# Hybrid decoder layer with routed experts: the end as products for gathered rows and last experts, smaller tiles, quarter refills, and unread products on TensorE while routing is worked out

## The chip, the cores and the metric

One core of a Trainium2 chip runs the whole program. The metric is the device time of one execution in microseconds; of several runs the median is given. Beside it one execution was profiled, and all rows below are from that one.

## The reference

One layer of a decoder on 512 tokens of width 1024 in float32: a mixer with four head groups, then a mixture of experts, then a last norm. The change touches only the mixture and what follows it:

```
lg = t @ w_rg + b_rg                       # 4 groups, the best one is taken
le = (t @ w_re + b_re) inside that group   # 4 experts, the best two are taken
w1, w2 = softmax weights of the two, times that of the group
y = sum over the two of  w * ((silu(t @ w_gate[e]) * (t @ w_up[e])) @ w_down[e])
x = x + g2 * y
out = rms_norm(x, final_norm)
```

Here `t` is the normed and modulated `x` (512 x 1024), `w_gate[e]` and `w_up[e]` are 1024 x 512 and `w_down[e]` is 512 x 1024. There are 16 experts, so each token's two rows make 1024 rows in all, spread unevenly over the experts.

## The kernel before

Each engine has its own instruction stream, written out by hand, with semaphores between them. The mixture begins in `pe_moe`, `act_moe`, `dve_moe`, `pool_moe` and `sync_moe`, with one function for each step of an expert. In what follows P = 128, ST = 4 (token tiles), KT = 8, E = 16.

**Routing.** For each of the four token tiles TensorE makes the output projection, transposes `x2` (L1196) and multiplies with the routing weights (L1203). Then VectorE picks group and experts (L1342 to L1381) and signals `before_tile`; TensorE counts how many rows of each expert stand before each token (L1208, L1209: the rank products); VectorE turns this into places (L1388 to L1447). The rows of the first expert are taken by products with 0/1 matrices (L1215), since they are on the chip; VectorE and ScalarE modulate them (`dve_rows`, `act_rows`, L1110 and L1078), and the first expert's products begin. For the other experts POOL gathers rows from DRAM by a list (L1540).

**Ranks and tiles.** The experts 0, 1 and 2 are pinned to the ranks 0 to 2 so that their weights can be loaded before routing is known. The others are ranked by their count of rows. A rank has a fixed number of rows, `SIZES`: 128 for ranks 0 to 7, 64 for 8 to 11, 32 for 12 to 15. What doesn't fit goes to up to 12 extra tiles of 128 rows behind the experts, each run only if it is needed (`extras`). `ORDER` is the order in which ranks are computed: 0, 1, 2, 14, 3, 13, 4, 12, 5, 11, 6, 10, 7, 9, 8, 15. "n" below is the place in that order.

**One expert.** `pe_gate_up` (L1031, small tiles L1025) makes gate and up, ScalarE the silu, VectorE the product, `pe_hidden` (L1041) transposes, `pe_down` (L1064, small tiles L1059) multiplies with the down weights, `dve_output` (L1131, L1135) multiplies with the gate `g2` into `yo`, and `act_output` (L1100) stores `yo` in DRAM. In TensorE's order the gate and up products of n come before the down products of n - 1, except for the last n.

**Weights.** SP loads them into three buffers. Gate and up of n wait for the gate and up products of n - 3, the down weights for the down products of n - 3. Only for n = 3 are gate and up loaded in quarters, each when a quarter of the first expert's products is done (L962); for all others L898. All weight loads are in one queue and are served in its order.

**The end.** When all stores but the last are through, POOL gathers each token's first row from DRAM (`y1`, four gathers, L1552), and after the last store its second (`y2`). VectorE adds `w1 * y1` (L1515) and `w2 * y2` (L1521), ScalarE makes the sum of squares (L1312) and the root (L1314), VectorE the mean (L1525), the reciprocal and the last product (L1528), and SP sends the tile out (L986). `fnb` (L974) is the last norm's weight.

## Time and profile before

| | us |
|---|---|
| median of 3 runs | 781.9 (779.35 to 783.69) |
| the profiled execution: time | 781.9 |
| the profiled execution: span | 780.0 |
| TensorE busy | 686.8 (88%) |
| VectorE busy | 318.2 (41%) |
| ScalarE busy | 180.0 (23%) |
| GpSimd busy | 116.7 (15%) |
| mean granted TensorE clock | 0.946 |
| first expert's products begin | 489.56 |
| last expert's products end | 747.95 |

The span is the time from the first to the last instruction; the time of an execution is 1.9 us longer. Engines: PE is TensorE (PEld its weight loads), DVE VectorE, ACT ScalarE, POOL GpSimd, SP the engine that only issues transfers; a name with q (SPq, ACTq) is that engine's sequencer. Busy shares are averages over stages with different limits, so one stage is read at a time. A float32 product shows as two records. A granted clock of 1.00 is 2.4 GHz, 0.50 is 1.2 GHz. DMA is the mean busy share of the 16 DMA engines; it can show a little over 1.

### The profile page before, as it was taken

How to read it: one execution, taken by the hardware profiler on the slowest of the kernel's cores; microseconds unless marked ns; L12 is line 12 of the kernel's file. 1: busy time of each engine (PE TensorE's matmuls, PEld its weight loads, DVE VectorE, ACT ScalarE, POOL GpSimd, SP SyncE). 2: the span in 40 equal slices, each digit the busy share in tenths (PEclk: the TensorE clock that was granted, in tenths of full speed). 3: DMA queues.
4: the chain of work that ended last, by engine and by line, in shares of the span. 5: the costliest groups of instructions: out<-in, count | busy, mean ns of one | idle time of the engine just before them, and what ended most of it. 6: DMA issues, size and time to landing. Idle time of an engine off the chain costs nothing.

```text
span 780.0 us, 9903 instructions
## 1 busy us (share of the span) xinstructions
PE 686.8 (88%) x3851; PEld 401.5 (51%) x3851; DVE 318.2 (41%) x752; ACT 180.0 (23%) x434; POOL 116.7 (15%) x164
## 2 busy tenths in 40 slices
PE   1799899999999999879999985899999999999830
PEld 1674446667666697545654455444444544443210
DVE  3203657856466533786612228350211211202126
ACT  3204215122121121456711141020111211201103
POOL 8700122313032155000000000010000000000030
PEclk9989999999999999899999986999999999999975
DMA  9999003793330300750085047638999999999965
GB/s 332 375 264 364 3 1 108 245 294 109 108 108 1 52 5 7 266 216 2 1 324 108 28 179 280 195 110 349 375 423 413 405 413 409 390 404 410 421 208 201
DMA packets 75475, 173.62 MB, mean 223 GB/s; under 512 B 21954, under 2 KB 38940, under 8 KB 71836
## 3 DMA queue, kind: packets, MB, share of 16 engines
q1 hardware_dynamic: 69520, 157.59, 56.0%
q0 software_dynamic: 2672, 9.44, 3.5%
q10 hardware_dynamic: 3228, 5.84, 2.0%
q8 instruction: 37, 0.61, 0.3%
q14 instruction: 18, 0.15, 0.1%
HBM read 156.59 MB, written 16.26 MB: 222 GB/s over the span
## 4 chain that ended last, share of the span: by engine, by line
PE 76%; DVE 9%; POOL 4%; issue 4%; ACT 3%; DMA 3%; POOLq 0%; ACTq 0%; DVEq 0%
PE ps L1031 14%; PE ps L1153 7%; PE ps L1064 7%; PE ps L2300 7%; PE ps L2267 5%; PE ps L1025 4%; PE ps L1059 2%; PE ps L2378 2%; PE ps L2264 2%; PE ps L2384 2%; DMA expert_rows<-yo 2%; PE ps L2291 2%; POOL lev L1648 2%; PE ps L653 2%; PE ps L2388 2%
## 5 line engine op out<-in xcount | busy, mean ns | idle before, releaser
L1031 PE MATMUL ps<-gu,xgT 128*128 128x512 f32 x256 | 113.0, 600 | 3.6 <-DVE xgT L1110 2.5
L1031 PEld LDWEIGHTS ps<-gu,xgT 128*128 128x128 f32 x256 | 48.6, 192 | 63.2 <-issue 63.2
L2300 PE MATMUL ps<-hT,winr 128*128 128x512 f32 x144 | 72.6, 612 | 0.0
L1540 POOL DMA_INDIRECT xg<-xn_rows,list x15 | 13.9, 928 | 384.7 <-DVE list L1447 185.9
L1153 PE MATMUL ps<-wout,yT 128*128 128x512 f32 x128 | 57.6, 610 | 0.0
L1064 PE MATMUL ps<-dn,hidT 128*128 128x512 f32 x128 | 56.5, 594 | 0.0
L1753 POOL TENSOR_TENSOR cc<-low,lev 128x512 f32<-128x512 f32 x20 | 30.2, 1518 | 129.5 <-DVE low L2087 104.0
L1891 DVE SCALAR_TENSOR_TENSOR acc<-ada,st,acc 128x512 f32<-128x512 f32 x56 | 48.5, 866 | 1.3
L2267 PE MATMUL ps<-hT,wind 128*128 128x512 f32 x96 | 43.4, 605 | 0.0
L1025 PE MATMUL ps<-gu,xgT 128*32 128x256 f32 (+1 forms) x384 | 43.0, 452 | 0.0
L1153 PEld LDWEIGHTS ps<-wout,yT 128*128 128x128 f32 x128 | 24.6, 195 | 30.0 <-issue 30.0
L1120 DVE TENSOR_TENSOR hidm<-sg,ps 128x512 f32<-128x512 f32 x8 | 5.5, 687 | 84.3 <-ACT sg L1085 84.3
L1085 ACT ACTIVATE sg<-ps 128x512 f32<-128x512 f32 (+2 forms) x16 | 7.4, 464 | 135.3 <-PE ps L1031 102.9
L1064 PEld LDWEIGHTS ps<-dn,hidT 128*128 128x128 f32 x128 | 23.7, 190 | 26.9 <-issue 26.8
L2300 PEld LDWEIGHTS ps<-hT,winr 128*128 128x128 f32 x144 | 24.0, 192 | 14.3 <-issue 12.3
L2267 PEld LDWEIGHTS ps<-hT,wind 128*128 128x128 f32 x96 | 18.4, 196 | 20.8 <-issue 20.7
L1135 DVE TENSOR_TENSOR yo<-ps,g2m 128x512 f32<-128x512 f32 x16 | 10.3, 687 | 45.3 <-PE ps L1064 27.8
L1025 PEld LDWEIGHTS ps<-gu,xgT 128*32 128x32 f32 (+1 forms) x384 | 16.7, 119 | 22.8 <-issue 18.0
L727 DVE TENSOR_REDUCE st<-ps 128x1 f32<-128x256 f32 (+3 forms) x48 | 20.3, 451 | 18.4 <-PE ps L660 18.3
L2101 DVE TENSOR_TENSOR uu<-uu,ps 128x512 f32<-128x512 f32 x20 | 13.7, 686 | 32.9 <-PE ps L2384 32.8
L1059 PE MATMUL ps<-dn,hidT 128*32 128x256 f32 (+1 forms) x192 | 24.0, 474 | 3.4 <-ACT hidT L1090 3.4
L780 ACT ACTIVATE pr<-ps,st 128x256 f32<-128x256 f32 (+3 forms) x48 | 23.5, 492 | 14.1 <-DVE st L727 14.1
(433 smaller groups left out, 1046.6 us busy)
## 6 DMA issues: line engine op xcount, KB each, us to landing
dn<-in_w_down SPq DMA_DIRECT2D x16, 2048.0 KB, 23.3
gu<-in_w_gate SPq DMA_DIRECT2D x15, 2048.0 KB, 21.5
gu<-in_w_up SPq DMA_DIRECT2D x15, 2048.0 KB, 26.0
ada<-in_w_ada SPq DMA_DIRECT2D x12, 2048.0 KB, 11.6
expert_rows<-zero SPq DMA_DIRECT2D x12, 512.0 KB, 6.7
expert_rows<-yo ACTq DMA_DIRECT2D x8, 512.0 KB
wout<-in_w_out SPq DMA_DIRECT2D x1, 3072.0 KB, 10.6
x<-in_x SPq DMA_DIRECT2D x2, 1024.0 KB, 6.2
```

Of the source, the lines that this page charges most:

```text
L653: t.matmul(PS[n][:, 0:nk], q[pb, pr, i * P:(i + 1) * P], keys[pb, 0, j0 * P:j0 * P + nk], start=True, stop=False)
L727: ins = v.tensor_reduce(m, PS[n][:, 0:nk], AX.X, ALU.max, negate=True)
L780: a.activation(T["pr"][:, u % PRS, 0:nk], PS[n][:, 0:nk], ACT.Exp, bias=m, accum_out=den[:, c:c + 1]).then_inc(sem("exp"), 1)
L1025: ins = nc.tensor.matmul(PS[2 * b][m * s:m * s + m, 0:2 * f].rearrange("p (w f) -> p w f", w=2), T["xgT"][:, k, 0:m], w_in[:, :, k, s * f: ...
L1031: ins = nc.tensor.matmul(PS[2 * b + w][:, :], T["xgT"][:, k, :], w_in[:, w, k, :], start=(k == 0), stop=(k == KT - 1))
L1059: ins = nc.tensor.matmul(PS[4][m * w:m * w + m, 0:d], T["hidT"][:, c, m * s:m * s + m], w_in[:, f, w * d:(w + 1) * d], start=(f == 0), sto ...
L1064: ins = nc.tensor.matmul(PS[4 + w][:, :], T["hidT"][:, f, :], w_in[:, f, w * 512:(w + 1) * 512], start=(f == 0), stop=(f == FT - 1))
L1153: ins = nc.tensor.matmul(PS[2 * (i % 2) + n][:, :], T["yT"][:, k, i * P:(i + 1) * P], T["wout"][:, k, n * 512:(n + 1) * 512], start=(k == ...
L1753: g.tensor_tensor(CC[lv % 2][:], T["low"][:], T["lev"][:, lv].unsqueeze(1).broadcast_to([P, H, P]), ALU.mult).then_inc(sem("cc"), 1)
L1891: ins = v.scalar_tensor_tensor(o, piece[:, k, :], csil[:, k:k + 1], o, ALU.mult, ALU.add)
L2267: ins = t.matmul(bank[:, :], w(k), T["hT"][:, k, :], start=(k == 0), stop=(k == KT - 1))
L2300: ins = t.matmul(bank[:, :], w(k), T["hT"][:, k, :], start=(k == 0), stop=(k == KT - 1))
```

## The change

- **Tile sizes.** `SIZES` is 128 for ranks 0 to 6, 64 for 7 to 11, 32 for 12 to 15. The last three in the order are the ranks 13, 14 and 15: the order is 0, 1, 2, 12, 3, 11, 4, 10, 5, 9, 6, 8, 7, 13, 14, 15. Up to 13 extra tiles.
- **Last three experts on chip** (`on_chip`). Their outputs go into the tile `yc` (96 rows) and are neither stored nor gathered.
- **The end as products** (`pe_back`). For each token tile TensorE adds up, in two PSUM banks, diag(w1) times `y1`, diag(w2) times `y2`, and a 0/1 matrix with weights (`back`) times `yc`: six products of 128 x 512. VectorE adds the result to `x2`. `back` is made by VectorE (`in_row`), transposed by TensorE (`pe_onehot`) and copied by ScalarE during the expert loop.
- **Gathers.** `y1` is gathered once the stores up to n = 11 are through and the gate and up products of n = 13 are done, `y2` after the store of n = 12.
- **Quarter refills** for n = 3, 4 and 5.
- **Unread products** (`keep_busy`): 11 products of 128 x 512 ahead of the rank products, 3 ahead of the first expert's row products, 3 ahead of its gate and up products. Nothing reads what they give.
- **Small steps.** The mean and epsilon of the norms move from VectorE into ScalarE's root; the root's table is loaded ahead of the last norm; the extra tiles' branches stand inside one outer branch; one more tile of zeros and a 64-row one are written to DRAM early.

```diff
-SIZES = [128] * 8 + [64] * 4 + [32] * 4
+SIZES = [128] * 7 + [64] * 5 + [32] * 4
+CHIP = 3
+_big, _less = list(range(NBUF, BIG)), list(range(E - CHIP - 1, BIG - 1, -1))
+while _big:
+    ORDER += [_less.pop(0), _big.pop(0)]
+ORDER += _less + list(range(E - CHIP, E))
+ONEHOT_AT = 3
...
-                if n == NBUF:
+                if n < 2 * NBUF:
+                    b = n - NBUF
                     for part in range(4):
                         if part < 3:
-                            sp.wait_ge(sem("first_gu_mm"), part + 1)
+                            sp.wait_ge(sem("first_gu_mm"), 3 * b + part + 1)
                         else:
-                            sp.wait_ge(sem("gu_mm"), 1)
+                            sp.wait_ge(sem("gu_mm"), b + 1)
...
+    def pe_back(pe):
+
+        pe.wait_ge(sem("routing"), ROUTING["route_i"])
+        pe.wait_ge(sem("exp_out"), 3)
+        pe.wait_ge(sem("diag"), 1)
+        pe.wait_ge(sem("y1_in"), 16 * ST)
+        for i in range(ST):
+            if i == 2:
+                pe.wait_ge(sem("yo_d"), E + 1)
+            for n in range(2):
+                if n:
+                    pe.wait_ge(sem(f"y_in{i}"), 16)
+                for w in range(2):
+                    nc.tensor.matmul(PS[2 * i + w][:, :], T[f"diag{n + 1}"][:, i, :],
+                                     T[f"y{n + 1}"][:, i, w * 512:(w + 1) * 512], start=(n == 0), stop=False)
+            pe.wait_ge(sem("yo_d"), E + 1)
+            for w in range(2):
+                ins = nc.tensor.matmul(PS[2 * i + w][:, :], T["back"][:, i * P:(i + 1) * P],
+                                       T["yc"][:, w * 512:(w + 1) * 512], start=False, stop=True)
+            ins.then_inc(sem("oproj_mm"), 1)
...
+        if on_chip(n):
+
+            dve.wait_ge(sem("yo_d"), E - CHIP + 1)
+            dve.wait_ge(sem("xg_tr"), E)
+            to = slice(32 * (n - E + CHIP + 1), 32 * (n - E + CHIP + 2))
+            for w in range(4):
+                rows, c = slice(32 * w, 32 * w + 32), slice(256 * w, 256 * w + 256)
+                ins = nc.vector.tensor_tensor(T["yc"][to, c], PS[down_bank(n)][rows, 0:256], T["g2q"][rows, :],
+                                              ALU.mult)
+            ins.then_inc(sem("yo_d"), 1)
+            return
...
+        def keep_busy(n):
+
+            for _ in range(n):
+                t.matmul(PS[0][:, :], idf[:], T["x2"][:, 0, 0:512], start=True, stop=True)
+
+        keep_busy(11)
         pe.wait_ge(sem("routing"), ROUTING["before_tile"])
...
+        keep_busy(3)
         pe.wait_ge(sem("routing"), ROUTING["first_rows"])
...
+        keep_busy(3)
         pe_gate_up(pe, 0, 0)
...
+            if n - 1 == ONEHOT_AT:
+                pe_onehot(pe)
...
         pe_hidden(pe, E - 1, 1)
         pe_down(pe, E - 1)
+        pe_back(pe)
...
+        for i in range(ST):
+            dve.wait_ge(sem("oproj_mm"), ST + i + 1)
+            for w in range(2):
+                x = T["x2"][:, i, w * 512:(w + 1) * 512]
+                ins = v.tensor_tensor(x, PS[2 * i + w][:, :], x, ALU.add)
+            ins.then_inc(sem("x3"), 1)
...
-            dve.wait_ge(sem("ss"), 2 * ST + i + 1)
-            v.tensor_scalar(ss[:, c], ss[:, c], 1.0 / D, EPS, ALU.mult, ALU.add).then_inc(sem("var"), 1)
...
         pool.wait_ge(sem("routing"), ROUTING["slots"])
-        pool.wait_ge(sem("yo_st"), 16 * STORED[E - 1])
+        pool.wait_ge(sem("gu_mm"), E - CHIP + 1)
+        pool.wait_ge(sem("yo_st"), 16 * STORED[E - CHIP - 1])
         for i in range(ST):
             rows_back(0, "y1_in", i)
...
-        pool.wait_ge(sem("yo_st"), 16 * STORED[E])
+        pool.wait_ge(sem("yo_st"), 16 * STORED[E - CHIP])
         for i in range(ST):
             rows_back(1, f"y_in{i}", i)
```

## Rows read from the trace of the kernel before

**Rows 1.** The page's slices (40 of 19.5 us, tenths busy): TensorE and DMA.
```profile
PE   1799899999999999879999985899999999999830
...
DMA  9999003793330300750085047638999999999965
```

**Rows 2.** Windows: length, busy us per engine (PE PEld DVE ACT POOL), clock, DMA share, GB/s.
```profile
511.50:524.00 12.50, 12.50 (x34) 5.75 (x34) 5.37 (x33) 0.45 (x1) 0.00 (x0) 1.00 0.01 5
...
579.05:745.05 166.00, 162.50 (x805) 71.42 (x804) 28.40 (x73) 25.00 (x67) 8.15 (x9) 0.99 1.01 407
745.50:746.50 1.00, 0.63 (x13) 0.31 (x16) 0.00 (x0) 0.28 (x1) 0.00 (x0) 1.00 0.01 2
749.00:757.00 8.00, 0.00 (x0) 0.00 (x0) 0.42 (x1) 0.00 (x0) 1.89 (x3) 0.57 0.77 276
```

**Rows 3.** Timeline of SP's queue: start, length, line, what is issued.
```profile
720.84 0.38 SPq L901 DMA_DIRECT2D dn<-in_w_down  x1
728.08 0.34 SPq L974 DMA_DIRECT2D fnb<-in_final_norm  x1
```

**Rows 4.** DMA issues by kind: size, median us from issue to landing.
```profile
fnb<-in_final_norm SPq DMA_DIRECT2D x1, 512.0 KB, 17.3
```

**Rows 5.** Timeline of TensorE: products of 128-, 64- and 32-row experts, and the end.
```profile
545.97 7.13 PE L1064 MATMUL ps<-dn,hidT 128*128 128x512 f32 x16
...
653.70 13.90 PE L1031 MATMUL ps<-gu,xgT 128*128 128x512 f32 x32
...
668.17 3.65 PE L1059 MATMUL ps<-dn,hidT 128*64 128x512 f32 x16
...
672.34 7.09 PE L1025 MATMUL ps<-gu,xgT 128*64 128x512 f32 x32
...
735.66 5.35 PE L1059 MATMUL ps<-dn,hidT 128*64 128x512 f32 x16 [3.06 <-ACT hidT L1090]
740.95 3.66 PE L1025 MATMUL ps<-gu,xgT 128*32 128x256 f32 x64
...
746.02 1.93 PE L1059 MATMUL ps<-dn,hidT 128*32 128x256 f32 x32 [0.37 <-ACT hidT L1090]
```

**Rows 6.** Chain (store) and timelines of VectorE, POOL, ScalarE, with idle time before.
```profile
722.22 11.01 DMA expert_rows<-yo
...
733.36 0.69 DVE L1131 TENSOR_TENSOR yo<-ps,g2s 128x512 f32<-128x512 f32 x1 [3.55 <-DMA expert_rows<-yo]
...
746.83 0.94 POOL L1552 DMA_INDIRECT y<-expert_rows,slot  x1 [43.78 <-DMA expert_rows<-yo]
...
750.03 0.42 DVE L1131 TENSOR_TENSOR yo<-ps,g2q 128x256 f32<-128x256 f32 x1 [4.76 <-remote]
...
773.53 1.04 ACT L1312 ACTIVATE sqs<-x 128x1024 f32<-128x1024 f32 x1
...
775.67 1.29 DVE L1528 SCALAR_TENSOR_TENSOR x<-x,st,fnb 128x1024 f32<-128x1024 f32 x1
```

**Rows 7.** Timeline of TensorE while routing is worked out.
```profile
463.62 3.60 PE L1203 MATMUL ps<-wrA,x2T 128*128 128x20 f32 x16 [1.17 <-ACT x2T L1270]
474.22 0.71 PE L1208 MATMUL ps<-chosen,before 128*128 128x80 f32 x2 [6.99 <-DVE earlier L1381]
...
477.31 8.94 PE L1215 MATMUL ps<-in_row,x 128*128 128x128 f32 x64 [1.95 <-DVE in_row L1393]
...
489.56 15.67 PE L1031 MATMUL ps<-gu,xgT 128*128 128x512 f32 x32 [2.52 <-DVE xgT L1110]
```

**Rows 8.** Windows of half a microsecond, columns as in the second group.
```profile
467.00:467.50 0.50, 0.23 (x2) 0.11 (x1) 0.16 (x3) 0.48 (x2) 0.00 (x0) 0.50 1.11 401
480.00:480.50 0.50, 0.50 (x5) 0.50 (x4) 0.45 (x2) 0.00 (x0) 0.00 (x0) 0.50 1.15 492
480.50:481.00 0.50, 0.50 (x6) 0.50 (x6) 0.43 (x4) 0.00 (x0) 0.00 (x0) 0.96 0.92 393
```

**Rows 9.** The tile `xg` from 480 us on: its 15 gathers, issue to landing.
```profile
DMA to landing us min/median/max: 4.5/9.7/11.9
```

More of the change, by code:

```diff
@@ L188, in sbuf_map @@
     o2 = at("r16", o2, [P, ST, E])
+    at("back", o2 + 2 * K, [P, S])
+    at("diag1", o2, [P, ST, P])
     o2 = at("in_row", o2, [P, 2, ST, P])
@@ L300, in build @@
     one = stat("one", 1)
+    eps = stat("eps", 1)
     rmod = stat("rmod", 2, KT)
@@ L874, in build @@
     gu, dn = [T[f"gu{b}"] for b in range(NBUF)], [T[f"dn{b}"] for b in range(NBUF)]
-    ORDER = list(range(NBUF))
-    big, less = list(range(NBUF, BIG)), list(range(E - 2, BIG - 1, -1))
-    while big:
-        ORDER.append(less.pop(0))
-        ORDER.append(big.pop(0))
-    ORDER += less + [E - 1]
-    LAST = ORDER[-1]
     def rows_of(n):
@@ L1014, in pe_gate_up @@
         w_in = gu[buffer_of(n)]
-        pe.wait_ge(sem(f"gu_in{buffer_of(n)}"), 32 * loads_of(n) + (96 if n >= NBUF and not buffer_of(n) else 0))
+        pe.wait_ge(sem(f"gu_in{buffer_of(n)}"), 32 * loads_of(n) + (96 if n >= NBUF else 0))
         pe.wait_ge(sem("xgT_a"), n + 1)
@@ L1136, in dve_output, with extra_count, extras @@
         ins.then_inc(sem("yo_d"), 1)
-    def extras(eng, body):
+    def extra_count(eng):
         eng.wait_ge(sem("routing"), ROUTING["route_i"])
-        n_extra = eng.value_load(T["route_i"][0:1, 0:1], min_val=0, max_val=EXTRA)
-        for x in range(EXTRA):
-            with eng.If(n_extra > x):
-                body(x, E + x)
-        return n_extra
+        return eng.value_load(T["route_i"][0:1, 0:1], min_val=0, max_val=EXTRA)
+    def extras(eng, n_extra, body, last=None):
+        with eng.If(n_extra > 0):
+            for x in range(EXTRA):
+                with eng.If(n_extra > x):
+                    body(x, E + x)
+            if last:
+                last()
     Y_ORDER = (0, 1, 6, 7, 2, 3, 4, 5)
@@ L1252, in extra @@
             pe_down(pe, n)
-        extras(pe, extra)
+        extras(pe, n_extra, extra)
     def act_moe(act):
@@ L1294, in act_moe @@
                 act_rows(act, n + 1)
+            if n - 1 == ONEHOT_AT:
+                act.wait_ge(sem("routing_pe"), ROUTING_PE["list_mm"] + 1)
+                a.activation(T["back"][:], PS[5][:, :], ACT.Copy).then_inc(sem("exp_out"), 1)
+            if not on_chip(n - 1):
                 act_output(act, n - 1)
+            if n == 3:
+                n_extra = extra_count(act)
         act_hidden(act, E - 1, 1)
-        act_output(act, E - 1)
-        act.wait_ge(sem("yo_zero"), 16 * EXTRA)
         def extra(x, n):
@@ L1304, in extra @@
             act_hidden(act, n, 0)
+            if n == E:
+                act.wait_ge(sem("yo_zero"), 16 * (EXTRA + 1))
             act_output(act, n)
-        extras(act, extra)
+        extras(act, n_extra, extra, lambda: act.wait_ge(sem("x3"), 2 * ST))
+        a.activation(rden[:, 0:1], one, ACT.Sqrt)
         for i in range(ST):
@@ L1420, in dve_moe @@
                 link(v.tensor_scalar(pad, order, n - 0.5, less, ALU.is_gt, ALU.mult))
-        link(v.tensor_scalar(t16, order, E - 1.5, float(OTHER_ROWS - sum(SIZES[:E - 1])), ALU.is_gt, ALU.mult))
+        link(v.tensor_scalar(t16, order, E - CHIP - 0.5, float(CHIP_ROW - EXTRA_ROW), ALU.is_gt, ALU.mult))
+        link(v.tensor_tensor(tile0, tile0, t16, ALU.add))
+        link(v.tensor_scalar(t16, order, float(MID), float(MID_ROW - ZERO_ROW), ALU.is_equal, ALU.mult))
         link(v.tensor_tensor(tile0, tile0, t16, ALU.add))
@@ L1492, in dve_moe @@
         link(v.tensor_scalar(T["rf"][:, 1:1 + EXTRA], T["rf"][:, 1:1 + EXTRA], float(E - 1), None, ALU.min))
-        v.tensor_copy(T["route_i"][:, 0:1 + EXTRA], T["rf"][:, 0:1 + EXTRA]).then_inc(sem("routing"), 1)
+        link(v.tensor_copy(T["route_i"][:, 0:1 + EXTRA], T["rf"][:, 0:1 + EXTRA]))
+        for i in range(ST):
+            ins = v.tensor_scalar(T["diag2"][:, i, :], idf[:], w2[:, i:i + 1], None, ALU.mult)
+        ins.then_inc(sem("routing"), 1)
+        n_extra = extra_count(dve)
         for n in range(1, E):
@@ L1500, in dve_moe @@
                 dve_output(dve, n - 1)
-        dve_output(dve, E - 1)
+            if n == E - 2:
+                v.memset(T["yc"][0:32, :], 0.0)
+            if n == ONEHOT_AT + 1:
+                dve.wait_ge(sem("routing_pe"), ROUTING_PE["list_mm"] + 1)
+                for i in range(ST):
+                    ins = v.tensor_scalar(T["diag1"][:, i, :], idf[:], w1[:, i:i + 1], None, ALU.mult)
+                ins.then_inc(sem("diag"), 1)
+        dve_output(dve, E - 1)
+        for i in range(ST):
+            dve.wait_ge(sem("oproj_mm"), ST + i + 1)
[3 more added lines that the diff above has]
+            ins.then_inc(sem("x3"), 1)
         def extra(x, n):
@@ L1689, in _ @@
         link(g.iota(T["row_i"][:], pattern=[[1, P]], base=0, channel_multiplier=0))
-        edges = [0] + STEPS_DOWN + [E - 1, E, E + EXTRA]
-        runs = [(a, b, (SIZES + [P] * EXTRA)[a]) for a, b in zip(edges, edges[1:])]
+        runs, a = [], 0
+        while a < E + EXTRA:
+            b, step = a + 1, max(1, (TILE_START + [0])[a + 1] - TILE_START[a])
+            while b < E + EXTRA and TILE_START[b] - TILE_START[b - 1] == step:
+                b += 1
+            runs.append((a, b, step))
+            a = b
         for a, b, step in runs:
```

126 lines of the change are left out of this document (85 added, 41 removed).

## The prediction

> **What bounds the kernel now.** I read the page's slices first. From 520 to about 735 us the PE row stands at 9, and from about 550 to 745 us so does the DMA row [rows 1]. Two full rows side by side mean that one hides the other, so the question is which of them has room. The windows answer it: the DMA engines idle from 511.5 to 524 us (share 0.01), and later there is no hole left: 1.01 at 407 GB/s over the 166 us from 579.05 to 745.05, and 0.01 right behind [rows 2]. The last down weights are issued at 720.84 us and `fnb` behind them at 728.08 us [rows 3]. `fnb` lands 17.3 us after its issue [rows 4], at 745.4 us. It is 0.52 MB, 1.2 us at that rate, so the last weights landed at about 744 us, and TensorE used them at 746.02 us [rows 5]. The expert loop is therefore bound twice: TensorE never idles until 732.6 us, and the weights arrive with 2 us to spare. Work taken from TensorE alone brings nothing unless bytes leave too.
>
> Behind the last products (747.95 us) lie 32 us: the stores, four gathers of `y1` and four of `y2`, sums and norms [rows 6].
>
> **Part 1, tile sizes and order.** Rank 7 gets 64 rows where it had 128, and the ranks 12 to 15 keep 32. A 128-row expert costs TensorE 13.90 + 7.13 us, a 64-row one 7.09 + 3.65 [rows 5], and I allow 0.6 us for the transposes of twice the columns: 10.9 us less. The stall of 3.06 us and the 1.7 us that the next down product took over its usual 3.65 (5.35, at half clock) [rows 5] go too, as the last three experts store nothing. TensorE alone would thus finish 15.7 us earlier, near 732. It can't use that, because the weights are the same 6.29 MB an expert (three transfers of 2048 KB, on the page). From the reference's own inputs, counted by me: the experts pinned to ranks 0 to 2 have 44, 121 and 101 rows, the others in order 127, 116, 106, 66, 62, 62, 57, 57, 37, 21, 19, 18, 10. Rank 7 has 62, so no extra tile arises.
>
> **Part 2, quarter refills.** They can fill the hole at 511.5 [rows 2]. But the load of the seventh expert's gate and up (n = 7) waits for the products of n = 4, which end at 579.05 us, before and after. What is gained is only the backlog that stands there. From 579.05 to 745.05 at 407 GB/s, 67.6 MB moved. I can name 66.0: nine gate-up pairs and ten down matrices (58.7), gathers of 704 rows of 4 KB (2.9), stores of 960 rows (3.9), `fnb` (0.5). The backlog was 1.6 MB. After the change only 9.6 MB are left for the time from 555.5 us, where the down weights of n = 4 may follow the products of n = 1 (now 553.1 us [rows 5]): two down matrices, one gate-up pair and 1.2 MB of rows. They take 23.5 us, up to 579.0, and n = 7 comes at 581.3. The backlog is gone: 3.8 us gained.
>
> **Part 3, unread products.** The logits' products end at 467.2 us, and the rank products start at 474.22 us, released by VectorE [rows 7]: a hole of 7.0 us. A 128x512 product is two records, 13.90 / 16 = 0.87 us [rows 5]. Eleven take 9.6 us at full clock. But the granted clock is 0.50 there, its half level (1.2 GHz), and when products began at that level at 477.31 us [rows 7] it rose at about 480.5 [rows 8], 3.2 us later. With about 3.1 us at half, 1.8 products are done and 9.2 remain: they end at 478.2 us. TensorE's queue is in order: the rank products wait behind them, and VectorE's whole routing chain behind those. Rank products run 0.5 us quicker, and VectorE has two more operations of 0.21 us. The first expert's products start 4.0 us later, at 493.5 us. For that they run at full clock, 13.90 and not 15.67 us [rows 5, 7], so all behind them is late by 2.2 us. The second group (3 products, 2.6 us against a hole of 1.95) delays products that VectorE's chain hides up to 488 us; the third fills the hole of 2.52 us [rows 7] and ends with VectorE. Bounds: -1.0 us (the clock high from the start) and +10 us (never rising while they run).
>
> The Trainium skill, TensorE: Matmul & The Clock Gate, section "Part 1: The HAM clock gate", says that the throttled state is the default and activity releases it. That speaks for these products; the trace agrees: the first expert's products took 15.67 us after a pause, those of a later one without a pause 13.90 [rows 5, 7]. By that rule alone this part would give 1.8 us instead of costing 2.2.
>
> **Part 4, gathers moved.** The `y1` gathers now need the store of the twelfth expert, and `y2` that of the thirteenth (a 64-row tile). The products of the thirteenth end at about 720 us, and a store in this stage took 11.0 us [rows 6]. So `y1` is fetched from about 722 and `y2` from about 732 us, both before the last weights. They are 1024 rows of 4 KB, 4.2 MB, 10.3 us at 407 GB/s. A gather from POOL during the saturated stage landed after 9.7 us median against 4.5 at best [rows 9]: it does get served among the weights, at their expense. No row shows four at once. At the least they cost the weights nothing (served after them); at the most 11.7 us, at the 358 GB/s of the tail (276 at a share of 0.77 [rows 2]). I take 10.3, as the gathers on POOL's queue were served promptly.
>
> The Trainium skill, DMA: Bandwidth & Descriptors, section "Issuing engines are not separate DMA queues", says that transfers started by any engine run on the same 16 DMA engines and interleave. It speaks against this move, and the landing times of [rows 9] agree. By the opposite reading the time would be the second rival's.
>
> Fewer rows are gathered (608) and stored (832, the last three experts none): 0.9 MB, 2.3 us less.
>
> **The sum.** n = 7 is issued at 579.05 + 2.2 = 581.3 us. 58.7 + 2.5 + 3.4 + 4.2 = 68.8 MB at 407 GB/s take 169 us: the last down weights land at 750.3 us, 6.4 later than now. The last gate and up land 5.2 us earlier, at 745.1. TensorE, idle since about 729, starts at half clock: 3.66 us + 1.7 (the surplus of 735.66 us). Then 1.4 us as now up to the down products, 1.93 us [rows 5]: the end is 753.8 us, 5.9 later than 747.95.
>
> **The new tail.** 24 products of 0.87 us take 20.9 us. The four before the first wait (3.5 us) hide VectorE's four writes to `yc` (0.42 us each [rows 6]), and the gathered rows are there by 747. Then two additions of 0.69 us, and the last norm, 3.4 us from the square to its end [rows 6] less 0.5 for the VectorE step that goes; 3.0 us for the last output transfer as now. 753.8 + 20.9 + 1.5 + 2.9 + 3.0 = 782.1 us. The tail is 28.3 us and was 32.0; that is what replacing stores and gathers by products brings.
>
> The span was 780.0 us, its execution 781.9, which is also the median: 1.9 us around it. So 784.0 us.
>
> At nothing I cost: the one-hot transposes, `diag` products and `back` copy (some 5 us on VectorE beside the second expert's 14 us of products, and 0.5 us on TensorE, which now waits for weights anyway); branches and the `Sqrt` table load moved ahead of the tail; 0.8 MB more of zeros near 150 us, where TensorE is full with other work [rows 1]. Uncovered they'd cost 1 to 2 us together.
>
> **Rivals.**
> (a) The unread products fit in: the clock is high when they start or VectorE is later than I read. 3.2 us less: 780.8. For it: the 6.99 us hole; against: the half clock at 467.
> (b) The gathers take nothing from the weights: these end at 740.0, the products at 743.7, and 743.7 + 28.3 + 1.9 = 773.9. For it: the weights' queue is deep and POOL's is small. Against: rows 9.
> (c) TensorE is the bound after all: 780 - 15.7 + 2.2 - 3.7 = 762.8, so 764.7. Against it the full DMA share.
> (d) Slower: the clock doesn't rise during the first group. Eleven products at 1.74 us end at 486.4, and the chain is late by 8.2 us more: 792. It decides if the granted clock is still at half at 475 us. For it: 3.6 us of logits' products ran through at half level [rows 7] without raising it. Against: these were products of 20 columns; with those of 128 columns it rose after 3.2 us [rows 8].
> (e) An extra tile arises after all (weights, gather, products, a second fetch): 45 us or more, near 830.
>
> **How the numbers follow.** The sum 0.45 (own range 780.5 to 788.5, from the bounds of the rate, 400 to 412 GB/s over 169 us, and the unread products), (a) 0.17, (b) 0.18, (c) 0.05, (d) 0.12, (e) 0.03. A measurement tells 0.5%, 3.9 us, from no change: 778.0 to 785.8. Faster are (b) and (c), 0.23. Same are (a) and 0.25 of the sum's 0.45, together 0.42. Slower are the other 0.20, (d) and (e), 0.35. The range goes down to (b) and up to where (d) begins: 772 to 791.
>
> **What would show it.** Right: DMA share near 1 up to about 750 us; TensorE idle for 10 us or more before the last 32-row expert's gate and up products, waiting for `gu`; gathers from 722; the rank products some 4 us later. Wrong: last weights landing before 743, TensorE without a hole to the end, or the rank products at 474 to 475 us. If the back products take over 0.87 us each, the tail is wrong.

## The result and the profile after

The changed kernel takes 791.9 us (median of 4 runs, 789.5 to 794.1) against 781.2 us for the kernel before (4 runs on the same chip): a ratio of 1.0163, 95% interval 1.0127 to 1.0200. It is slower by 10.7 us. Forecast were 784.0 us and 772 to 791; the time lies just above the range. Of all the runs behind this document two are left out of every median and ratio, one of 1111 us of the kernel before with its tail changed and one of 1744 us of the first kernel of "both together".

The profiled execution of the changed kernel took 794.1 us with a span of 791.9 us, 11.9 us more than the span before of 780.0. The page's slices, 40 of 19.8 us each (tenths busy; the middle row is the granted clock):

```profile
PE   1699899999999998889999989899999999999384
...
PEclk9789999999999999889998979999999999999698
DMA  9999003993330302550282065788899999999932
```

As in [rows 1], PE and DMA are both full from slice 30 on. New are the 3 in the PE row and the 6 in the clock row at the same place (slice 38, 732.5 to 752.3 us). Of the two weak DMA slices at the end the first still holds the end of the weights, up to 759 us; only in the second are output transfers all that is left.

TensorE while routing is worked out (timeline: start, duration, engine, line, operation, tile; in brackets the idle time before it and what released it), which answers [rows 7]:

```profile
465.57 3.60 PE L1265 MATMUL ps<-wrA,x2T 128*128 128x20 f32 x16 [1.17 <-ACT x2T L1349]
469.01 12.54 PE L1271 MATMUL ps<-x,idf 128*128 128x512 f32 x22
481.38 0.34 PE L1276 MATMUL ps<-chosen,before 128*128 128x80 f32 x2
...
492.36 2.82 PE L1271 MATMUL ps<-x,idf 128*128 128x512 f32 x6
...
496.59 13.97 PE L1048 MATMUL ps<-gu,xgT 128*128 128x512 f32 x32 [1.41 <-DVE xgT L1156]
```

The eleven unread products take 12.5 us in a hole that was 7.0 us. The rank products of L1276 stand right behind them without any idle time, 12.2 us after the logits' products end (469.17) and not 7.0.

Windows around the stretch that the weights fill (length; busy time of PE, PEld, DVE, ACT, POOL; granted clock; DMA share; GB/s), which answer [rows 2]. 584.38 us is the moment at which the weights of the seventh expert, n = 7, are issued; I call it t7:

```profile
576.00:584.38 8.38, 8.38 (x24) 3.56 (x23) 0.00 (x0) 0.14 (x1) 0.00 (x0) 1.00 0.99 408
584.38:594.38 10.00, 10.00 (x80) 4.31 (x78) 2.91 (x10) 2.83 (x7) 0.91 (x1) 1.00 0.93 299
584.38:759.20 174.82, 157.44 (x809) 67.69 (x807) 31.71 (x83) 26.50 (x71) 15.58 (x17) 0.95 1.01 398
```

The DMA engines are full for 174.8 us behind t7 at 398 GB/s, 69.6 MB, and TensorE is busy for 157.4 us of them. Before it was 161.9 of 165.0 us (a window from 579.05 to 744.00 us there, 408 GB/s). The end on TensorE, which answers the end of [rows 5]:

```profile
737.84 3.47 PE L1076 MATMUL ps<-dn,hidT 128*32 128x256 f32 x32 [3.87 <-issue]
750.16 5.85 PE L1042 MATMUL ps<-gu,xgT 128*32 128x256 f32 x64 [8.85 <-DMA gu<-in_w_up]
...
759.25 1.94 PE L1076 MATMUL ps<-dn,hidT 128*32 128x256 f32 x32 [2.17 <-issue]
761.11 3.70 PE L1106 MATMUL ps<-y,diag 128*128 128x512 f32 x8
...
780.10 1.88 PE L1110 MATMUL ps<-yc,back 128*128 128x512 f32 x4
```

TensorE waits 8.85 us for the last `gu` and then for the last `dn` ("issue" names no releaser; the window from 759 to 760 us has a DMA share of 0.22 and the next one 0.00, so the last bytes land as these products begin). The 24 products behind (eight of L1106 and four of L1110 here are records of two per product) run without a gap. VectorE at the end (same columns):

```profile
782.02 1.29 DVE L1615 TENSOR_TENSOR x<-ps,x 128x512 f32<-128x512 f32 x2 [3.86 <-PE ps L1110]
783.22 0.15 DVE L1645 RECIPROCAL st<-st 128x1 f32<-128x1 f32 x1
783.41 1.28 DVE L1646 SCALAR_TENSOR_TENSOR x<-x,st,fnb 128x1024 f32<-128x1024 f32 x1
784.61 0.15 DVE L1645 RECIPROCAL st<-st 128x1 f32<-128x1 f32 x1
784.80 1.28 DVE L1646 SCALAR_TENSOR_TENSOR x<-x,st,fnb 128x1024 f32<-128x1024 f32 x1
...
787.40 0.16 DVE L1645 RECIPROCAL st<-st 128x1 f32<-128x1 f32 x1
787.59 1.29 DVE L1646 SCALAR_TENSOR_TENSOR x<-x,st,fnb 128x1024 f32<-128x1024 f32 x1
```

All four norms stand in a row behind the last sum, though three of the tiles were summed 5 to 15 us earlier. POOL's gathers of `y` (timeline; before they began at 746.83 us, [rows 6]), and the DMA issues of the stretch 440 to 792 us (transfers, KB each, median us from issue to landing):

```profile
724.89 0.94 POOL L1670 DMA_INDIRECT y<-expert_rows,slot  x1 [12.28 <-DMA expert_rows<-yo]
...
733.58 0.94 POOL L1670 DMA_INDIRECT y<-expert_rows,slot  x1 [4.02 <-DMA expert_rows<-yo]
```

```profile
y<-expert_rows,slot POOLq DMA_INDIRECT x8, 18.4
...
fnb<-in_final_norm SPq DMA_DIRECT2D x1, 512.0 KB, 29.5
```

So the 11.9 us of span divide into four, by the points that both traces have:

| stretch | before | after | difference |
|---|---|---|---|
| start to the end of the logits' products | 467.2 | 469.2 | +2.0 |
| from there to t7 | 111.8 | 115.2 | +3.4 |
| t7 to the end of the last down products | 168.9 | 176.8 | +7.9 |
| from there to the end (tail) | 32.0 | 30.7 | -1.3 |

(By rounding the rows add up to 12.0.) The first row isn't the change's: the logits' last group of products starts at 459 to 466 us in all the kernels run here, those of before's kind and of after's alike. The two traces are 0.3 us apart at 422 us and 2.0 us at 459 us. Between them lies the output projection, where 32 records took 16.67 us after and 13.98 before (the granted clock from 424 to 428 us was 0.50 and 1.00), and the next 32 took 13.98 and 15.68.

The last row needs care too. Four other kernels below have the tail of the kernel before, unchanged, and in their traces it takes 30.1 to 30.7 us and not 32.0. In the trace of before the last scaling into `yo` starts 2.1 us behind the last products (750.03 us, [rows 6]), in those four 0.1 to 0.8 us behind them. The changed kernel's tail takes 30.7 to 30.8 us in four traces (31.5 and 31.7 in two more, whose first `y` products run at half clock). So replacing stores and gathers by products made the tail hardly shorter, if at all; the -1.3 us are mostly this one trace of before. The times below are therefore given from t7 where they can be: "D" is the end of the last down products.

### The profile page after: what moved, and what is told of

Read it like the earlier page. It is cut to its first block, busy times and chain, and to the rows that moved or that the text cites. A ratio compares the mean times of both kernels' runs of the same rounds, so it can differ in the third digit from the quotient of the medians.

```text
span 791.9 us, 10083 instructions
## 1 busy us (share of the span) xinstructions
PE 715.7 (90%) x3935; PEld 411.0 (52%) x3935; DVE 321.4 (41%) x779; ACT 180.5 (23%) x436; POOL 116.8 (15%) x165
## 4 chain that ended last, share of the span: by engine, by line
PE 77%; DVE 8%; DMA 4%; POOL 4%; ACT 3%; issue 3%; SPq 0%; POOLq 0%; DVEq 0%; ACTq 0%
PE ps L1048 12%; PE ps L1215 7%; PE ps L2432 7%; PE ps L1081 6%; PE ps L1042 6%; PE ps L2399 5%; DMA gu<-in_w_up 4%; PE ps L1076 2%; PE ps L2510 2%; PE ps L2516 2%; PE ps L2396 2%; PE ps L2423 2%; POOL lev L1774 2%; PE ps L1106 2%; PE ps L2520 2%
## 5 line engine op out<-in xcount | busy, mean ns | idle before, releaser
L1048 PE MATMUL ps<-gu,xgT 128*128 128x512 f32 x224 | 97.4, 593 | 2.5 <-DVE xgT L1156 1.4
L1048 PEld LDWEIGHTS ps<-gu,xgT 128*128 128x128 f32 x224 | 42.0, 190 | 54.0 <-issue 54.0
L1042 PE MATMUL ps<-gu,xgT 128*32 128x256 f32 (+1 forms) x416 | 52.3, 488 | 8.8 <-DMA gu<-in_w_up 8.8
L1081 PE MATMUL ps<-dn,hidT 128*128 128x512 f32 x112 | 49.4, 594 | 0.0
L1042 PEld LDWEIGHTS ps<-gu,xgT 128*32 128x32 f32 (+1 forms) x416 | 19.6, 127 | 37.2 <-issue 23.5
L1076 PE MATMUL ps<-dn,hidT 128*32 128x256 f32 (+1 forms) x208 | 29.7, 527 | 7.8 <-issue 7.8
L1081 PEld LDWEIGHTS ps<-dn,hidT 128*128 128x128 f32 x112 | 20.7, 190 | 23.5 <-issue 23.4
L2318 PE MATMUL ps<-ada,st 128*32 128x128 f32 x256 | 11.2, 339 | 19.1 <-DMA ada<-in_w_ada 18.4
L1164 DVE TENSOR_TENSOR hidm<-sg,ps 128x256 f32<-128x256 f32 (+1 forms) x9 | 3.3, 362 | 60.8 <-ACT sg L1131 60.8
## 6 DMA issues: line engine op xcount, KB each, us to landing
gu<-in_w_up SPq DMA_DIRECT2D x13, 2048.0 KB, 22.3
```

The lines of the kernel that those rows point to most:

```text
L1042: ins = nc.tensor.matmul(PS[2 * b][m * s:m * s + m, 0:2 * f].rearrange("p (w f) -> p w f", w=2), T["xgT"][:, k, 0:m], w_in[:, :, k, s * f: ...
L1048: ins = nc.tensor.matmul(PS[2 * b + w][:, :], T["xgT"][:, k, :], w_in[:, w, k, :], start=(k == 0), stop=(k == KT - 1))
L1076: ins = nc.tensor.matmul(PS[down_bank(n)][m * w:m * w + m, 0:d], T["hidT"][:, c, m * s:m * s + m], w_in[:, f, w * d:(w + 1) * d], start=(f ...
L1081: ins = nc.tensor.matmul(PS[4 + w][:, :], T["hidT"][:, f, :], w_in[:, f, w * 512:(w + 1) * 512], start=(f == 0), stop=(f == FT - 1))
```

## The experiments

Each kernel starts from the kernel before (names with b) or from the changed one (names with a). All compute the full output, with unread products beside it where the text says so. Ratios are to the kernel before on the same chip, with 95% intervals. They aren't the quotients of the two medians, which differ from them by up to 0.2%. Where two kernels are compared with each other, their ratios are subtracted; kernels with the same median of before in the text ran side by side.

**The changed kernel again, and without the unread products.**

```
-        keep_busy(11)
...
-        keep_busy(3)     (both)
```

> The changed kernel without any of the 17 unread products. Theory (they push the rank products out by 5.2 us and give 1.7 us back in the first expert): rank products 7.0 us after the logits instead of 12.2, the first expert's products back to 15.6 us, the load for n = 7 some 3.3 us earlier, and the whole 3.3 us shorter, since the last weights come that much earlier: 788.6. Rival (the warm clock is worth more than the push): 1.8 us longer, 793.7. Second rival (the loss is all at the end): unchanged, 791.9.

> The changed kernel itself, on the chip of this group, so that the others can be held against it. From the recorded ratio 1.0163: 12 to 13 us over the kernel before.

Without them: 786.5 us, 1.0113 [1.0081, 1.0145]. The changed kernel, run again later, took 791.0 us, 1.015 [1.011, 1.019]. In the trace without them the rank products start 7.0 us after the logits again, the first expert takes 15.6 us and not 14.0, and the logits' end to t7 is 112.2 us, where it is 115.2 with them. By these traces the unread products cost about 3 us, some 0.4%; the ratios differ by 0.4 to 0.5%, with overlapping intervals. About two thirds of the loss have other causes.

**The unread products alone, in the kernel before.**

```
+        keep_busy(11)
         pe.wait_ge(sem("routing"), ROUTING["before_tile"])
...
+        keep_busy(3)     (before the first rows, and before pe_gate_up(pe, 0, 0))
```

> The kernel before with the 17 unread products and nothing else. Theory: 5.2 us later at the rank products, 1.7 us back in the first expert, so 3.3 to 3.5 us longer: 785.3 against 781.9. Rival (the warm clock pays): 1.8 us shorter, 780.1.

779.8 against 777.2 us, 1.0035 [1.0015, 1.0056]: 2.7 us. The same price from the other side: the logits' end to t7 is 114.7 us instead of 111.8. t7 to D is 168.0 us and not 168.9, so nothing shows that the rest of the loop hides this delay.

**Gathers that wait for the last weights.**

```
         pool.wait_ge(sem("gu_mm"), E - CHIP + 1)
+        pool.wait_ge(sem(f"dn_in{(E - 1) % NBUF}"), 16 * ((E - 1) // NBUF + 1))
```

> The changed kernel with the eight gathers of y1 and y2 held back until the last down weights have landed. Theory (the gathers take their bytes from the weights): the last down weights land 10 us earlier than now, at about 749 instead of 759 us, and the last expert's gate and up products start at about 744 instead of 750; the whole stays near 791 us, because the gathers are then at the end, where they take some 12 us. Rival (the gathers are served from what the weights leave): the last weights still land at 759 us and the whole is longer by the gathers, 803.

790.5 against 777.2 us, 1.0176 [1.0152, 1.0200]. TensorE, POOL (timelines):

```profile
737.71 5.49 PE L1042 MATMUL ps<-gu,xgT 128*32 128x256 f32 x64 [6.22 <-DMA gu<-in_w_up]
...
744.63 1.93 PE L1076 MATMUL ps<-dn,hidT 128*32 128x256 f32 x32 [0.37 <-ACT hidT L1136]
753.21 6.32 PE L1106 MATMUL ps<-y,diag 128*128 128x512 f32 x8 [6.65 <-DMA y<-expert_rows,slot]
```

```profile
743.59 0.94 POOL L1670 DMA_INDIRECT y<-expert_rows,slot  x1 [37.18 <-PE ps L1042]
```

With t7 at 578.17 us, POOL could start at t7+165.4, so the last weights were there by then; they were there at t7+174.8 with the gathers among them. The gathers take at least 9.4 us from the weights. Behind the weights they cost the same again: TensorE waits 6.65 us for rows and then runs its first eight records in 6.32 us instead of 3.70. t7 to the end is 208.5 us against 207.5. So it matters little where in this stage the 4.2 MB are moved; what matters is that the last weights wait for them or they for the last weights.

**The old tile sizes in the changed kernel.**

```
-SIZES = [128] * 7 + [64] * 5 + [32] * 4
+SIZES = [128] * 8 + [64] * 4 + [32] * 4
```

> The changed kernel with the tile sizes of before (eight tiles of 128 rows, four of 64, four of 32; the extra 64 rows are in n = 12): 10.9 us more work on TensorE, 0.5 MB more to move. Theory (the weights bound the end, TensorE idles 15 us there): 1 to 3 us longer, 793 to 795, with TensorE's idle time before the last expert gone. Rival (TensorE is the bound): 10.9 us longer, 803.

Expected were 1 to 3 us more; it came out faster. 787.0 us, 1.0114 [1.0087, 1.0140] beside the two runs above with 777.2 us for before. t7 to D is 174.4 us, 2.4 less than with the smaller tiles, and t7 to the end 205.8 against 207.5. The interval overlaps that of the changed kernel (1.015, below 1.0163), so the medians say that 10.9 us more work on TensorE cost nothing, and the traces that they gain some 2 us. The trace shows a reason: TensorE reaches the stores later, the `y2` gathers start at 742.5 us (t7+161.3) and not at 733.6 (t7+149.2), and the last `gu` has landed before they share the DMA engines:

```profile
741.80 3.66 PE L1042 MATMUL ps<-gu,xgT 128*32 128x256 f32 x64 [2.46 <-DMA gu<-in_w_up]
...
751.89 3.64 PE L1076 MATMUL ps<-dn,hidT 128*32 128x256 f32 x32 [5.37 <-issue]
```

The last down products start at t7+170.7 and not at t7+174.9, and the DMA engines go on at 401 to 418 GB/s for 2 us behind that, where they stand still in the changed kernel: a part of the gathers' bytes now comes behind the last weights. About 1.7 us of it is lost again, as these down products run at half clock (3.64 us and not 1.94). All this stands on one trace of each.

**The new tile sizes in the kernel before.** The same edit the other way.

> The kernel before with the new tile sizes and nothing else (order 0, 1, 2, 14, 3, 13, 4, 12, 5, 11, 6, 10, 7, 9, 8, 15): 10.9 us less on TensorE, the same weights. Theory (the weights arrive with 2 us to spare): 0 to 3 us shorter, with TensorE idle before the last experts. Rival (TensorE alone is the bound): 10.9 us shorter.

776.7 against 778.5 us, 0.9984 [0.9959, 1.0009]; t7 to D is 168.6 us, and 168.9 in the kernel before. Work taken from TensorE alone brings nothing that can be measured. The trace shows that this has two causes:

```profile
740.88 5.35 PE L1025 MATMUL ps<-gu,xgT 128*32 128x256 f32 x64 [2.30 <-DMA gu<-in_w_up]
```

Of the 10.9 us the weights let through 2.0: the last gate and up products start at t7+159.9 and not at t7+161.9. Then they run at half clock for a while, 5.35 us and not 3.66, and 1.7 of the 2.0 us are gone.

**More work on TensorE.** Twelve unread products in the loop, behind the down products of n = 10, in both kernels:

```
+            if n in (11,):
+                for _ in range(12):
+                    nc.tensor.matmul(PS[2 * (1 - b)][:, :], idf[:], T["x2"][:, 0, 0:512], start=True, stop=True)
```

> The changed kernel with 12 unread products of 128 x 512 (10.4 us) more on TensorE, behind the down products of n = 10, in the midst of the expert loop. Theory (the weights' queue bounds the loop's end, TensorE has room): within 2 us of the changed kernel, TensorE's idle time before the last expert shorter by 10 us. Rival (TensorE is the bound): 10.4 us longer.

> The kernel before with the same 12 unread products (10.4 us) behind the down products of n = 10. If it is bound by both, as the prediction says, TensorE's time shows: its last products come 7 to 10 us later (the 3 us stall before the down products of n = 14 may be taken up) and the whole is 7 to 10 us longer, with a hole of as much in the DMA share. If only the weights bound it: 2 us or less.

They take 10.46 us in both traces. The changed kernel with them: 790.9 us, 1.0137 [1.0096, 1.0178], and t7 to D 177.1 us: nothing, beside 1.015 without them. The kernel before with them: 786.7 us, 1.0094 [1.0060, 1.0129], and t7 to D 176.5 us. 1.0094 is 7.3 us more than before, and t7 to D is 7.6 us longer. A window of it (columns as above) shows who is the bound there now:

```profile
745.00:755.00 10.00, 8.73 (x105) 3.90 (x109) 0.98 (x2) 0.69 (x3) 0.23 (x1) 1.00 0.21 48
```

The DMA engines are nearly idle and TensorE works. So the kernel before had about 3 us to spare on TensorE (10.5 added, 7.3 seen), and the changed one about 10 (its wait for the last `gu` is 2.65 us now and was 8.85): the change moved the end of the loop fully to the weights' queue. This is the test for a loop that looks full on both sides.

**Norms between the sums.** In the changed kernel without extra tiles:

```
+            sums(0)
+            for i in range(1, ST):
+                sums(i)
+                norm(i - 1, last_link)
+            norm(ST - 1, last_link)
```

> The changed kernel with the last norm of a token tile done by VectorE right behind the sum of the next tile, where no extra tile is needed, instead of all four norms behind all four sums. Theory (the tail is 30.7 us and not 28.3 since VectorE does the four norms in a row, 783.2 to 788.9 us, after the last sum): 2.4 to 2.8 us shorter. Rival (another thing, the root on ScalarE or the output transfers, sets the end): unchanged.

789.35 against 779.85 us, 1.0121 [1.0082, 1.0159]; beside 1.015 of the changed kernel the intervals overlap. In its trace the tail is 28.8 us and not 30.7, t7 to the end 205.6 us and not 207.5 to 208.0. The place is shown, its size of about 2 us by traces alone (30.7 to 30.8 us in four traces without this edit, 28.8 here).

**Whole refills.** Quarters for n = 3 only, as before:

```
-                if n < 2 * NBUF:
+                if n == NBUF:
```

> The changed kernel with quarter refills for n = 3 alone, as before the change; n = 4 and 5 load gate and up whole. Theory (the quarters only took up the backlog at n = 7): 3.8 us longer than the changed kernel, 795.7 of 791.9, with no dip of the DMA rate behind the issue for n = 7. Rival (the queue is full anyway from there): unchanged.

791.7 against 778.5 us, 1.0190 [1.0146, 1.0233]; t7 to D is 178.6 us (176.8 and 177.2 in the two traces of the changed kernel), t7 to the end 210.3 (207.5 and 208.0). By the traces the quarter refills bring 1.5 to 1.8 us up to D and 2.3 to 2.8 us to the end, where the first eight records of the `y` products took 4.59 us instead of 3.70. The ratio is 0.3 to 0.4% above the changed kernel's, with overlapping intervals, and I had given them 3.8 us. The 10 us from t7 on show what the old bytes did:

```profile
578.09:588.09 10.00, 10.00 (x80) 4.31 (x78) 2.90 (x10) 2.83 (x7) 0.91 (x1) 1.00 1.03 377
```

At 377 GB/s with a backlog of old bytes, at 299 GB/s without it (above): 0.8 MB, 1.9 us at 407 GB/s.

**The other steps in the kernel before.** First its own tail: `Sqrt` reads the sum of squares with scale and bias, so VectorE loses a step per tile, the root's table is loaded ahead, and the norm of a tile stands right behind the next tile's additions.

```
-            act.wait_ge(sem("var"), 3 + ST + i + 1)
-            a.activation(rstd[:, i:i + 1], ss[:, i:i + 1], ACT.Sqrt).then_inc(sem("sd"), 1)
+            act.wait_ge(sem("ss"), 2 * ST + i + 1)
+            a.activation(rstd[:, i:i + 1], ss[:, i:i + 1], ACT.Sqrt, scale=1.0 / D, bias=eps).then_inc(sem("sd"), 1)
...
+            for j in ([i - 1] if i < ST - 1 else [i - 1, i]) if i else []:
```

> The kernel before with the change's norm steps (mean and epsilon inside ScalarE's root, its table loaded ahead) and the norm of a tile done by VectorE right behind the sum of the next one. Theory: the last sum is at 769.7 us and the last norm then takes 2.9 us instead of ending at 776.96: 4 us shorter. Rival (VectorE's sums or the output transfers set it): 1 us or less.

775.4 against 778.5 us, 0.9979 [0.9949, 1.0009]: not told apart from before, where 4 us were expected. The tail is 28.2 us in the trace and 32.0 in that of before, but 30.1 to 30.7 us in the four other kernels with before's tail. So these steps bring some 2 us in the traces, and not the 3.8 that the two traces alone suggest. Then the same with the new sizes and the quarter refills:

> The kernel before with those norm steps and their order, the new tile sizes and the quarter refills for n = 3, 4 and 5; the gathers stay behind the last weights and there are no unread products. Theory: 4 us from the norms and 4 to 6 us from the loop, since backlog and TensorE's time are both cut: 8 to 10 us shorter than before. Rival (backlog is worth nothing): 4 us shorter.

776.2 against 778.5 us, 0.9973 [0.9939, 1.0006]. Expected were 8 to 10 us. The last gate and up products did start earlier, at t7+158.7, where the kernel with the tail alone has them at t7+161.6 and the one with the new sizes alone at t7+159.9; but TensorE, with nothing left to do, had fallen to the lower clock:

```profile
729.12 3.65 PE L1061 MATMUL ps<-dn,hidT 128*64 128x512 f32 x16 [2.04 <-ACT hidT L1092]
736.45 6.40 PE L1027 MATMUL ps<-gu,xgT 128*32 128x256 f32 x64 [3.67 <-DMA gu<-in_w_up]
```

6.40 us where a busy TensorE takes 3.66: 2.7 of the 2.9 us are given back. With the 2 us of the tail (28.0 us here) that is far from the 8 to 10 expected. (The granted clock is 0.56 over these 6.40 us.)

**Unread products in that wait.**

```
                 pe_down(pe, n - 1)
+                for _ in range(4):
+                    nc.tensor.matmul(PS[2 * (1 - b)][:, :], idf[:], T["x2"][:, 0, 0:512], start=True, stop=True)
             pe_gate_up(pe, n, b)
```

(for the last n alone)

> The previous combination on the kernel before (norm steps, new tile sizes, quarter refills) with 4 unread products (3.5 us) in the wait of TensorE for the last expert's gate and up weights. Theory (what the earlier weights brought was lost because TensorE had idled and did the last gate and up products in 6.40 us instead of 3.66): those back to 3.66 us, 2.7 us shorter than the combination, about 0.6% under before. Rival (the last down weights bound it anyway): unchanged, 0.3% under before.

776.6 against 779.1 us, 0.9968 [0.9940, 0.9995]. In the trace they do what they should: the last gate and up take 3.66 us again, and t7 to D is 165.8 us instead of 168.5. The medians of the two kernels can't be told apart, so the 2.7 us stand on one trace each. Up to the end only 1.0 us of them is left (t7 to the end 195.5 us and 196.5), since the tail of this trace is 29.7 us long and that of the other 28.0.

**Fewer unread products while routing is worked out:** 5, 2 and 2 instead of 11, 3 and 3, in the kernel before.

> The kernel before with few unread products, 5 ahead of the rank products, 2 and 2 ahead of the two others, where the change has 11, 3 and 3. Theory (they cost only what they overrun the hole, and what they give is the clock of the first expert): 5 products take 5.9 us of the 7.0 us hole, so the rank products aren't pushed; they run 0.4 us quicker and the first expert takes 13.97 us instead of 15.67: about 2 us shorter than before. Rival (unread products cost time as such): longer than before.

776.4 against 779.1 us, 0.9968 [0.9938, 0.9997]:

```profile
466.49 7.28 PE L1209 MATMUL ps<-x,idf 128*128 128x512 f32 x10
473.65 0.45 PE L1214 MATMUL ps<-chosen,before 128*128 128x80 f32 x2
```

Five end as the hole ends, and the rank products aren't late. Nine products give about 0.3% where seventeen cost 0.35%, though the interval ends just below 1. In this trace the first expert took 15.67 us as before, and what came of the nine is 0.5 us: its products start 21.9 us behind the logits' end and not 22.3. In the trace of the next kernel, with the same nine, it took 13.97 us, and t7 comes 109.7 us behind the logits' end where it was 111.8 before. In that of the last one it took 15.67 us again. So the nine can give 2.1 us, and in some executions give 0.5.

**Both together, in the kernel before and in the changed one** (there with the old sizes and the norms between the sums):

> Both together on the kernel before: the combination, 4 unread products in the last wait, and 5, 2 and 2 in the routing stage. Theory: 2 us under the version with only the 4, in all 6 to 7 us (0.8%) under before. Rival: the gains don't add up, since the weights bound the end, but as their first load starts earlier too, no less than the larger of the two.

> The changed kernel (on-chip end, gathers among the weights) with the tile sizes of before, 5, 2 and 2 unread products and the norms between the sums. Theory: 1.7 us (sizes), 5 us (the unread products no longer push: 3 us, and the rest as in the routing stage of before), 2.4 us (norms) shorter than the changed kernel: 782 to 784 where that is 791. It stays 0.2 to 0.5% above before, since the 9.5 us that the gathers take from the weights remain.

The first: 774.9 against 779.1 us, 0.9940 [0.9909, 0.9971], 0.6% faster than the kernel before and 2.2% than the changed one. Its first and its last experts:

```profile
485.53 13.97 PE L1033 MATMUL ps<-gu,xgT 128*128 128x512 f32 x32 [2.25 <-DVE xgT L1112]
...
729.30 3.70 PE L1249 MATMUL ps<-x,idf 128*128 128x512 f32 x8
732.93 3.66 PE L1027 MATMUL ps<-gu,xgT 128*32 128x256 f32 x64
...
738.01 1.93 PE L1061 MATMUL ps<-dn,hidT 128*32 128x256 f32 x32 [0.37 <-ACT hidT L1092]
```

The second: 781.9 us, 1.0027 [1.0000, 1.0053]. Three repairs take off 1.2 to 1.4% of the changed kernel's 1.5 to 1.6, and with them it is no faster than the kernel before. I read what is left as the price of the gathers among the weights; that was not tested by itself.

## Why the prediction was right and where it failed

**The bound: right.** The weights' queue sets the end of the loop. Ten more microseconds of TensorE work cost the changed kernel nothing, and ten fewer brought the kernel before nothing (the weights let through 2.0 us of them, and the clock took 1.7 back). Rival (c), TensorE as the bound, is refuted by both. That the kernel before is bound twice, with 2 to 3 us between, is shown by its 7.3 us for 10.5.

**Part 1, sizes: right that they bring nothing; the harm was missed.** In the changed kernel they bring the stores and with them the `y2` gathers forward into the weights that are needed last, and leave TensorE idle. That cost about 2 us, by the trace of the run with the old sizes, whose last down weights came 4 us earlier. The trade was in my text (`y2` "from about 732 us", measured 733.6), but I had priced the gathers' bytes alone and not their place. Rival (e), the extra tile, didn't happen.

**Part 2, quarter refills: mis-sized,** 1.5 to 2.8 us and not 3.8. I took the backlog away at the full rate and let the rate begin at 407 GB/s. Without a backlog the queue starts from empty, and the first 10 us run at 299 GB/s; 404 in the kernel before.

**Part 3, unread products: right mechanism, 3.0 to 3.4 us and not 2.2.** I had the rank products about 4 us late; they are 5.2 us late (12.2 against 7.0). The eleven products took 12.5 us and not 11.0, because the granted clock stayed at half longer than the 3.2 us that I had taken from [rows 7, 8]. Windows of the changed kernel, the products beginning at 469.01 us:

```profile
473.00:474.00 1.00, 1.00 (x2) 0.34 (x1) 0.85 (x5) 0.00 (x0) 0.00 (x0) 0.50 0.58 195
474.00:475.00 1.00, 1.00 (x3) 0.39 (x2) 0.86 (x6) 0.20 (x1) 0.00 (x0) 0.62 0.08 18
```

It rises near 474.8, 5.8 us after their start: 3.3 products at half, 7.7 at full, 5.8 + 6.7 = 12.5 us. The first expert's 1.7 us at full clock came as said (13.97 us). Rival (d), the clock at half through the whole group, was nearer than I thought (it was to decide at 475 us) and didn't happen; rival (a) neither. The rule that activity releases the clock (the Trainium skill, TensorE: Matmul & The Clock Gate, section "Part 1: The HAM clock gate") agrees with the 13.97 us here; but the order of the queue costs more than the clock gives.

**Part 4, gathers: right.** Taken from the weights: 9.4 us, forecast 10.3. Rival (b), gathers that cost the weights nothing, is refuted by the run in which they wait. (Its own sum has 743.7 us where its steps give 743.5.) The Trainium skill's sentence that transfers of all issuing engines share the 16 DMA engines (DMA: Bandwidth & Descriptors, section "Issuing engines are not separate DMA queues") is borne out by the same run.

**The sum: the term that failed is the weights' time,** 174.8 us behind t7 and not 169.0. Of the 5.8 us, 2.1 are bytes (69.6 MB and not 68.8; `fnb`'s 0.5 is a part, for I let it come behind the last weights, and its bytes move among them, landing after 29.5 us), and 3.7 are the rate, 398 GB/s and not 407. Of those, 2.6 us belong to the first 10 us: (404 - 299) GB/s over 10 us are 1.05 MB. The last `gu` at t7+165.8 was forecast for t7+163.8; the cold gate and up products, 5.85 us, for 5.4. The down products waited for `dn` where I had `gu` as the last wait, so the cold gate and up were hidden in the end: D lies 2.0 us behind the last weights and not 3.5.

**The tail: 30.7 us and not 28.3.** The 24 products took the 20.9 us of the sum. The step that failed is "the last norm, 3.4 us from the square to its end": I took the square at 773.53 in [rows 6] for one released by the last sum. The lines of VectorE in the kernel before show that it is not:

```profile
767.17 2.52 DVE L1521 SCALAR_TENSOR_TENSOR x<-y,w2t,x 128x1024 f32<-128x1024 f32 x2 [1.89 <-DMA y<-expert_rows,slot]
...
770.22 1.28 DVE L1528 SCALAR_TENSOR_TENSOR x<-x,st,fnb 128x1024 f32<-128x1024 f32 x1
...
772.04 1.29 DVE L1528 SCALAR_TENSOR_TENSOR x<-x,st,fnb 128x1024 f32<-128x1024 f32 x1
...
773.85 1.28 DVE L1528 SCALAR_TENSOR_TENSOR x<-x,st,fnb 128x1024 f32<-128x1024 f32 x1
```

The last sum ends at 769.7, and four norms follow one after the other, the last ending at 776.96: 7.3 us, of which I saw the last 3.4. After the change the four still stand in a row, from 783.3 to 788.9: 5.6 us where the sum had 2.9. That is 2.7 too little, less 0.2 at the two additions. Norms between the sums took 1.9 us of it away. The other half of that step, "the tail is 28.3 us and was 32.0; that is what replacing stores and gathers by products brings", rested on the one trace of before: beside the 30.1 to 30.7 us of the four others even 28.3 us would have been some 2 us, and 30.7 are nothing.

**Together:** the profiled execution took 794.1 us, 10.1 above the forecast: 2.0 before the logits' end, 1.1 for the unread products (t7 115.2 us behind the logits' end, where the sum had 114.1), 4.3 from t7 to D (the weights' 5.8 less the 1.5 by which D lay nearer to them), 2.4 in the tail and 0.3 around the span. The 2.0 us at the start aren't the change's; without them its time is 792.1, still above the range. No single rival came true: three terms of the likeliest case were each too small, by 1 to 4 us, and my range had bounds for the rate alone and none for the tail.

**What remains open:** why the same five, two and two unread products bring the first expert to full clock in one trace of three; why the last scaling into `yo` was late in the one trace of before; and whether the last wait's warm products bring anything on average, since the medians don't show it.

## What to carry to other kernels

In a loop that is full on two engines, add 10 us of idle work to one of them and see what comes out: that gives the slack that no busy row shows. Bytes that must be moved cost the same here before or behind the last weights, so bring forward only what fits into a hole, and don't finish compute early if that pulls stores and gathers into the transfers that are needed last. Fill an engine's hole with work that ends before the hole does (in an in-order queue each microsecond over is late for everyone), and place the last steps of a finished tile ahead of the next tile's wait. Hold a stage's time against several traces of kernels that share it before you call a difference of 1 to 2 us a gain.

## What the runs showed of the hardware

- A TensorE that has waited is slow again: products of 3.66 us took 5.85 and 6.40 after waits of 8.9 and 3.7 us, down products of 1.93 us took 3.47 after 3.9, the first `y` products 6.32 and not 3.70 after 6.65. Waits of about 2.4 us went either way: the last gate and up products took 3.66 us after 2.46 us (old sizes) and 5.35 after 2.30 (new sizes in the kernel before). In two kernels of before's kind this took back most of what the weights' earlier arrival gave: 1.7 of 2.0 us and 2.7 of 2.9.
- Eight gathers of 512 KB in the saturated stage landed after 18.4 us in the median, the same behind the weights after 6.0, and with the old sizes, where a part of their bytes came behind the weights, after 11.7.
- The DMA engines show a share of 0.93 at 299 GB/s in the first 10 us behind t7 and one of 1.03 at 404 there in the kernel before: the share alone doesn't tell the rate.
- The start of the logits' last products lies between 459 and 466 us, also in kernels that are the same up to there: 463.62 us in the kernel before, 459.25 in the one with the unread products behind them. In the pair before and after 1.7 us of this come from one stretch of the output projection in which the clock was at half in one and full in the other. On one trace of each, a difference under some 2 us means nothing unless it is taken from a point behind that.
